# Chunk loop of a hybrid SSD and DeltaNet block: state-space output computed by channels, corners only in the last substitution steps, decay rows requested from ScalarE

## The chip, the cores and the metric

One core of a Trainium2 chip runs the whole kernel. The metric is the device time in microseconds; for the kernel before it is the median of three runs. A profile of one execution goes with it.

## The reference

One layer (`DEPTH` = 1) on 1024 tokens of 1024 channels, all in float32. Only the part around the change is kept here.

```python
def ssd_chunked(xh, dt, a, bm, cm):                      # 16 heads of 64, 2 groups, state 128
    a_cum = jnp.cumsum(a_dt, axis=-1)
    lmat = jnp.exp(jnp.where(causal, a_cum[..., :, None] - a_cum[..., None, :], -jnp.inf))
    scores = jnp.einsum('bclgn,bcsgn->bcgls', cc, bc)
    y_diag = jnp.einsum('bcgrls,bcsgrp->bclgrp', scores[:, :, :, None] * lmat, xc)
    ...                                                  # states carried from chunk to chunk
    y_off = jnp.einsum('bclgn,bcgrpn,bcgrl->bclgrp', cc, prev, jnp.exp(a_cum))
    return (y_diag + y_off).reshape(bsz, s, h, pd)

# mamba2_branch: y = (y + d_skip * xh) * silu(z), then an RMS norm per group
# gated_delta_chunked, 8 heads of 128:
    sol = lax.linalg.triangular_solve(t_mat, rhs, left_side=True, lower=True, unit_diagonal=True)
    v_new = u_c - w_c @ state
    o = qd_c @ state + qk_c @ v_new
    state = state * last_c + kd_c.T @ v_new

# around it: proj = h @ w_in; two branch projections merged by sigmoid gates; w_out; a gated
# conv-MLP with D_FF = 4096; a gated per-layer input embedding; RMS norms between them
```

The kernel uses chunks of 128 tokens in place of 64; the recurrences give the same result.

## The kernel before

The program is written by hand for five engines, each with its own instruction stream; semaphores tie them together. `wait_ge` puts a wait in front of the next instruction of an engine. There is no scheduler: the order of the work is the order of the code. The helper `after(eng, s, count)` (L861) waits for a count of a semaphore that earlier stages have used already.

The large products (`w_in`, the branches, the MLP) are done as three fp32r products of a high and a low part, each 128x512; they fill most of the time. TensorE has such products through the chunk loop too: `gemm(steps)` (L1054) puts in steps of six of them, from the projection for the merge gates, between the small products of a chunk. A chunk has 12 steps in chunks 0 to 3 and 8 in chunks 4 to 7.

The chunk loop handles 8 chunks of 128 tokens (`NCH`). For a chunk `c`:

- SyncE (`sp_mixer`) requests all inputs: `gt` (gates), `qk`, `xbc` (x, B and C by channels), `bv`, `dec`, `kdec`, `mq`, `zt` (silu of z), and for the chunk after next `nt` and `dd`. `dec` is a broadcast: 16 rows of 128 cumulated decays are read for each of the 128 partitions (L921), 1 MB in pieces of 512 B.
- GpSimd (`pool_mixer`) subtracts the own token's sum from `dec` and masks it (`decays`, L988), scales x (`decayed_x`), decays the states, puts the skip term into `yssm` (`skip_x`), and splits weights.
- ScalarE (`act_mixer`) takes the exponential of `dec`, copies PSUM results (`rhs`, `rinv`, `bs`), squares, and has the Ln/Exp pairs for the norms. `mg_evict` takes a finished gate tile out of PSUM.
- VectorE (`dve_mixer`) multiplies `dec` with the scores (L1320), forms `rhs`, sums outputs and states, and multiplies by the norm factors (L1378 for the DeltaNet heads, L1384 for the state-space channels).
- TensorE (`pe_mixer`) does products of 8 or 16 heads at a time through the PSUM banks `PA`, `PB`, `PC` (two each).

The triangular solve is an inverse by blocks of 32. The inverses of the diagonal blocks come from an earlier stage (`dd`). In the loop, `invert_r` forms one factor `rinv`, and `invert_h` / `invert_x` apply it three times, each time 8 products of 128x128 on TensorE and two additions on VectorE (L1313), so that the blocks further from the diagonal fill in one step at a time.

The state-space output of a chunk is formed by tokens: `off_done` marks C times the state (L1121), which VectorE scales by the exponential of the sum (L1346) into `ysum`; `diag` (L1097) multiplies the masked scores of 8 heads with x, with two neighbouring heads' channels as the moving operand, half of which is thrown away by `add_diag` (L1322). It runs twice, since 8 heads fill the two banks. TensorE then transposes `ysum` (L1151) to channels, and VectorE adds it to `yssm` (L1369) and multiplies by `zt` (L1372).

The numbers of instructions that the text uses are those of the lines below.

## Time and profile before

| | |
|---|---|
| runs | 2536.34, 2541.39, 2546.09 us; median 2541.39 |
| span of the profiled execution | 2534.6 us |
| time of the profiled execution beyond its span | the profile gives none |
| busy: TensorE, VectorE, ScalarE, GpSimd | 96%, 61%, 32%, 50% |
| chunk loop with its start (740 to 1130 us) | 390 us of the span |

The span is the time from the first to the last instruction of one profiled execution; it is 6.8 us below the median of the runs. "Busy" adds up the time in which an engine works on something. A line such as `[0.64 <-DVE rhs L1337]` in the timeline says that the engine sat idle for 0.64 us before the instruction and that line 1337 on VectorE released it. Stretches are given in microseconds from the start of the span.

### The profile page before, as it was taken

The numbers are of one execution on the slowest core, as the hardware profiler recorded it, in microseconds if no ns is written. First come the engines' busy times: TensorE is split into PE (matmuls) and PEld (weight loads), VectorE is DVE, ScalarE is ACT, GpSimd is POOL, SyncE is SP. The second block draws the span as 40 slices with busy tenths as digits, with TensorE's granted clock in tenths as the row PEclk, the third lists the DMA queues.
The fourth block names the chain that finished last, engine by engine and source line by source line (L and its number), as shares of the span: only waits on it lengthen the run. The fifth ranks groups of instructions, "written<-read, shape, count | busy, mean of one in ns | idle before, by whom it ended". The sixth has DMA issues, their size and how long they took to land. (4 is left out here: it accounts for less than half of the span.)

```text
span 2534.6 us, 29658 instructions
## 1 busy us (share of the span) xinstructions
PE 2436.9 (96%) x11540; PEld 2011.4 (79%) x11540; DVE 1538.6 (61%) x1411; ACT 822.5 (32%) x965; POOL 1266.1 (50%) x687
## 2 busy tenths in 40 slices
PE   7999999899999999989999899999999999999998
PEld 6888887677778888878878678888888878888776
DVE  4977997325766567653244897677677652323575
ACT  5234443445412232331013543333333321000332
POOL 2337887544445455443353266556556543333563
PEclk9999999999999999999999999999999999999999
DMA  6222334698676667745232222222222243122332
GB/s 230 92 84 92 108 120 135 216 267 283 202 209 168 187 173 215 178 141 174 100 133 83 100 83 75 74 98 75 74 97 76 100 174 116 50 83 84 131 101 108
DMA packets 293607, 335.34 MB, mean 132 GB/s; under 512 B 44461, under 2 KB 249594, under 8 KB 289402
## 3 DMA queue, kind: packets, MB, share of 16 engines
q1 hardware_dynamic: 260650, 271.42, 34.4%
q10 hardware_dynamic: 32848, 62.40, 6.7%
q8 instruction: 76, 1.25, 0.2%
q14 instruction: 33, 0.27, 0.0%
HBM read 230.50 MB, written 103.28 MB: 132 GB/s over the span
## 5 line engine op out<-in xcount | busy, mean ns | idle before, releaser
L498 PE MATMUL ps<-act_hi,w_hi 128*128 128x512 f32 x1328 | 532.4, 401 | 13.3 <-ACT ring_b L1212 4.8
L483 POOL TENSOR_SCALAR w_hi<-w_raw 128x1024 fp32r<-128x1024 f32 x123 | 145.0, 1179 | 764.0 <-issue 688.4
L502 PE MATMUL ps<-act_hi,w_lo 128*128 128x512 f32 x1328 | 518.4, 390 | 0.0
L501 PE MATMUL ps<-act_lo,w_hi 128*128 128x512 f32 x1328 | 517.9, 390 | 0.0
L485 POOL TENSOR_TENSOR w_lo<-w_raw,w_hi 128x1024 fp32r<-128x1024 f32 x123 | 328.6, 2672 | 10.3
L498 PEld LDWEIGHTS ps<-act_hi,w_hi 128*128 128x128 f32 x1328 | 250.0, 188 | 71.6 <-issue 8.1
L502 PEld LDWEIGHTS ps<-act_hi,w_lo 128*128 128x128 f32 x1328 | 249.8, 188 | 53.1
L501 PEld LDWEIGHTS ps<-act_lo,w_hi 128*128 128x128 f32 x1328 | 250.1, 188 | 52.3 <-issue 3.3
L2036 POOL TENSOR_TENSOR w_lo<-sm,w_hi 128x512 fp32r<-128x512 f32 x120 | 209.1, 1743 | 113.9 <-ACT w_hi L2390 113.9
L2036 POOL TENSOR_TENSOR w_lo<-w_raw,w_hi 128x512 fp32r<-128x512 f32 x90 | 139.3, 1549 | 151.8 <-ACT w_hi L2390 151.8
L2152 PE MATMUL ps<-t,w_hi 128*128 128x512 f32 x480 | 186.9, 389 | 0.2 <-POOL w_lo L2036 0.2
L2153 PE MATMUL ps<-t,w_hi 128*128 128x512 f32 x480 | 186.8, 389 | 0.0
L2154 PE MATMUL ps<-t,w_lo 128*128 128x512 f32 x480 | 186.7, 389 | 0.0
L2152 PE MATMUL ps<-act_hi,w_hi 128*128 128x512 f32 x360 | 140.3, 390 | 3.2 <-DVE ring L2716 2.7
L2153 PE MATMUL ps<-act_lo,w_hi 128*128 128x512 f32 x360 | 140.1, 389 | 0.0
L2154 PE MATMUL ps<-act_hi,w_lo 128*128 128x512 f32 x360 | 140.1, 389 | 0.0
L2799 DVE TENSOR_TENSOR tile<-ps,tile 128x1024 f32<-128x1024 f32 x24 | 29.4, 1224 | 160.8 <-PE ps L502 133.8
L2390 ACT ACTIVATE w_hi<-sm 128x512 fp32r<-128x512 f32 x120 | 75.3, 630 | 133.0 <-PE ps L2154 133.0
L2464 ACT ACTIVATE act_hi<-f_raw 128x1024 fp32r<-128x1024 f32 x32 | 31.2, 1047 | 254.7 <-DMA f_raw<-f_cm 254.7
L579 POOL TENSOR_TENSOR w_lo<-csm,w_hi 128x512 fp32r<-128x512 f32 x48 | 93.3, 1953 | 34.6 <-ACT w_hi L648 34.5
L2152 PEld LDWEIGHTS ps<-t,w_hi 128*128 128x128 f32 x480 | 90.1, 188 | 19.3 <-POOL w_lo L2036 0.6
L2153 PEld LDWEIGHTS ps<-t,w_hi 128*128 128x128 f32 x480 | 90.1, 188 | 18.7
(393 smaller groups left out, 5130.9 us busy)
## 6 DMA issues: line engine op xcount, KB each, us to landing
w_raw<-in_w_in_dram SPq DMA_DIRECT2D x34, 1024.0 KB, 6.0
spill<-ring_a ACTq DMA_DIRECT2D x36, 512.0 KB, 2.6
w_raw<-in_w_ffn_down_dram SPq DMA_DIRECT2D x18, 1024.0 KB, 5.0
w_raw<-in_w_ffn_up_dram SPq DMA_DIRECT2D x16, 1024.0 KB, 5.2
w_raw<-in_w_ffn_gate_dram SPq DMA_DIRECT2D x16, 1024.0 KB, 5.2
f_cm<-ring SPq DMA_DIRECT2D x32, 512.0 KB, 2.6
spill<-ring_b ACTq DMA_DIRECT2D x31, 512.0 KB, 6.9
qkv_a<-spill SPq DMA_DIRECT2D x7, 1536.0 KB, 8.4
```

Source lines behind the costliest of these rows:

```text
L483: nc.gpsimd.tensor_scalar(hi, raw, 1.0, 0.0, ALU.mult, ALU.add).then_inc(split_done, 1)
L485: nc.gpsimd.tensor_tensor(lo, raw, hi.bitcast(f32), ALU.subtract).then_inc(split_done, 1)
L498: first = nc.tensor.matmul(o, wh, mov[0][:, k, c], start=(k == 0), stop=False)
L501: nc.tensor.matmul(o, wh, mov[1][:, k, c], start=False, stop=False)
L502: last = nc.tensor.matmul(o, wl, mov[0][:, k, c], start=False, stop=(k == KD - 1))
L579: nc.gpsimd.tensor_tensor(c_slot(w_lo, j), c_product_in(p, i), c_slot(w_hi, j).bitcast(f32), ALU.subtract).then_inc(c_low[0], 1)
L2036: nc.gpsimd.tensor_tensor(product_slot(w_lo, j), product_in(q, i), product_slot(w_hi, j).bitcast(f32), ALU.subtract).then_inc(w_low[0], 1)
L2152: nc.tensor.matmul(dst, wh[:, k, :], mh[:, k, :], start=(k == 0), stop=False)
L2153: nc.tensor.matmul(dst, wh[:, k, :], ml[:, k, :], start=False, stop=False)
L2154: last = nc.tensor.matmul(dst, wl[:, k, :], mh[:, k, :], start=False, stop=(k == 3))
L2390: a(product_slot(w_hi, j), product_in(q, i), ACT.Copy).then_inc(w_high[0], 1)
L2464: a(hi[:, k, :], raw[:, k, :], ACT.Copy).then_inc(f_hi_done, 1)
```

## The change

Four edits, all in the chunk loop or for it:

1. The state-space output is formed by channels. C times the state (now `s_ssm` of two heads as the stationary operand) gives channels by tokens, in 8 products. `diag` has the x of one head (64 channels) as the stationary operand and the masked scores as the moving one, even heads to PSUM partitions 0 to 63, odd heads to 64 to 127. All 16 heads fit into the two banks at once, so `diag` runs once, and the eight transposes of `ysum` go. VectorE multiplies by the exponential of the sums with channels on partitions, which needs these rows broadcast: a second scratch tensor `exp_rows` is written once before the loop, and SyncE loads it into `zt` ahead of each chunk's output (two transfers); `zt` is loaded a second time in the chunk, with z, once the product has been formed.
2. The second and third substitution step compute only the corner of the matrix that still changes, 64x64 and 32x32 per head, and VectorE copies the corner instead of adding the whole.
3. `dec` for the next chunk is requested by ScalarE, after the second `rhs` copy, once `diag` is done.
4. The semaphore counts follow (`x_step` 4 instead of 6 a chunk, `diag_done` 1 instead of 2, `y_sum` 2 instead of 3).

```diff
+    CORNER = {1: (slice(0, 64), 64), 2: (slice(0, 32), 32)}
+
+    def load_dec(eng, c):
+
+        after(eng, diag_done, c)
+        eng.dma_start(dec[:, :, :], cum_rows[ROW_DT:ROW_DT + SSM_HEADS, tokens(c)].unsqueeze(0).broadcast_to([P, SSM_HEADS, P])
+                      ).then_inc(in_dec, 16)
...
+        def load_e(c):
+            after(sp, y_mid, c * 2)
+            for i in range(2):
+                rows = exp_rows[ROW_DT + i:ROW_DT + SSM_HEADS:2, tokens(c)]
+                sp.dma_start(zt[64 * i:64 * i + 64, :, :], rows.unsqueeze(0).broadcast_to([64, KD, P])).then_inc(in_e, 16)
 
         def load_z(c):
-            after(sp, y_mid, c * 2)
+            after(sp, y_sum, c * 2 + 1)
             sp.dma_start(zt[:, :, :], spill_c[:, J_Z:J_Z + Z_T, tokens(c)]).then_inc(in_z, 16)
...
                 load_qk(c + 1)
                 load_xbc(c + 1)
                 load_bv(c + 1)
+            load_z(c)
             if c in blocks_at:
                 block_load(blocks_at[c])
             if c < NCH - 1:
-                load_dec(c + 1)
                 load_kd(c + 1)
                 load_mq(c + 1)
-                load_z(c + 1)
+                load_e(c + 1)
...
+            after(pe, x_step, c * 4 + nth + 1)
+            rows, n = CORNER[nth]
+            for h in range(GDN_HEADS):
+                last = t.matmul(bank(PB + nth - 1)[rows, h * n:(h + 1) * n], rinv[:, h, rows], xinv[:, h, P - n:P], start=True, stop=True)
+            last.then_inc(h_done, 1)
...
-        def diag(c, g):
-            for i in range(HPG):
-                h = g * HPG + i
-                last = t.matmul(bank(PB, 2)[:, i * P:(i + 1) * P], dec[:, h, :],
-                                xc[:, h - h % 2:h - h % 2 + 2, :].rearrange("p h d -> p (h d)"), start=True, stop=True)
+        def diag(c):
+            for h in range(SSM_HEADS):
+                d = slice(SSM_HEAD_DIM * (h % 2), SSM_HEAD_DIM * (h % 2) + SSM_HEAD_DIM)
+                last = t.matmul(bank(PB, 2)[d, h // 2 * P:(h // 2 + 1) * P], xc[:, h, :], dec[:, h, :], start=True, stop=True)
             last.then_inc(diag_done, 1)
...
-            after(pe, o_sum, c * 2 + 2)
-            for k in range(KD):
-                last = t.transpose(bank(PA, 2)[:, k * P:(k + 1) * P], ysum[:, k * P:(k + 1) * P], ident[:, :])
-            last.then_inc(yt_done, 1)
...
+            if more:
+                load_dec(act, c + 1)
             after(act, o_sum, c * 2 + 2)
...
+            if nth:
+                rows, n = CORNER[nth]
+                after(dve, h_done, c * 4 + nth + 2)
+                after(dve, x_step, c * 4 + nth + 1)
+                v.tensor_copy(xinv[rows, :, P - n:P], bank(PB + nth - 1)[rows, 0:GDN_HEADS * n].rearrange("p (h t) -> p h t", t=n)
+                              ).then_inc(x_step, 1)
+                return
...
-            v.tensor_tensor(hd(ysum[:, :]), hd(bank(PC, 2)), wide(head_cols(c, EXP_D, SSM_HEADS), SSM_HEAD_DIM),
-                            ALU.mult).then_inc(y_sum, 1)
-            after(dve, y_sum, c * 3 + 1)
-            add_diag(c, 0)
-            add_diag(c, 1)
+            after(dve, in_e, c * 32 + 32)
+            after(dve, y_mid, c * 2)
+            v.tensor_tensor(hd(ysum[:, :], KD), hd(bank(PC, 2), KD), zt[:, :, :], ALU.mult).then_inc(y_sum, 1)
+            after(dve, diag_done, c + 1)
+            after(dve, y_sum, c * 2 + 1)
+            v.tensor_tensor(ysum[:, :], bank(PB, 2), ysum[:, :], ALU.add).then_inc(y_sum, 1)
...
+            a(hrow[:, 0, :], hrow[:, 1, :], ACT.Exp).then_inc(tm_act, 1)
+            act.wait_ge(tm_act, 5)
+            act.dma_start(exp_rows, hrow[:, 0, :]).then_inc(cum_kept, 16)
```

How the streams stand. On TensorE, in a chunk of the second half of the loop, from the products with `rhs` (L1068, the new values) over `diag` (L1100) to the state update; before:

```order
L1068 MATMUL ps<-rhs,xinv 128x128 x8
L1100 MATMUL ps<-xc,dec 128x128 x8
L498 MATMUL ps<-act_hi,w_hi 128x512
L501 MATMUL ps<-act_lo,w_hi 128x512
L502 MATMUL ps<-act_hi,w_lo 128x512
L498 MATMUL ps<-act_hi,w_hi 128x512
L501 MATMUL ps<-act_lo,w_hi 128x512
L502 MATMUL ps<-act_hi,w_lo 128x512
L1100 MATMUL ps<-xc,dec 128x128 x8
L1068 MATMUL ps<-rhs,kdec 128x128 x8
```

and in the changed kernel, where `diag` is L1115 and the helper for products by head L1078:

```order
L1078 MATMUL ps<-rhs,xinv 128x128 x8
L1115 MATMUL ps<-dec,xc 64x128 x16
L499 MATMUL ps<-act_hi,w_hi 128x512
L502 MATMUL ps<-act_lo,w_hi 128x512
L503 MATMUL ps<-act_hi,w_lo 128x512
L499 MATMUL ps<-act_hi,w_hi 128x512
L502 MATMUL ps<-act_lo,w_hi 128x512
L503 MATMUL ps<-act_hi,w_lo 128x512
L1078 MATMUL ps<-rhs,kdec 128x128 x8
```

The sixteen products stand together, with 64 stationary columns each; the step of large products follows them. Further on in the same chunk, from the sum of squares (L1166) over the second and third substitution step to the transposes of the DeltaNet output (L1176); before:

```order
L1166 MATMUL ps<-sqs,ones 128x128 x8
L1068 MATMUL ps<-xinv,rinv 128x128 x8
L498 MATMUL ps<-act_hi,w_hi 128x512
L501 MATMUL ps<-act_lo,w_hi 128x512
L502 MATMUL ps<-act_hi,w_lo 128x512
L498 MATMUL ps<-act_hi,w_hi 128x512
L501 MATMUL ps<-act_lo,w_hi 128x512
L502 MATMUL ps<-act_hi,w_lo 128x512
L1068 MATMUL ps<-xinv,rinv 128x128 x8
L1176 MATMUL ps<-ident,qs 128x128 x8
```

and in the changed kernel (L1096 is the corner product, L1176 the sum of squares, L1186 the transposes):

```order
L1176 MATMUL ps<-sqs,ones 128x128 x8
L1096 MATMUL ps<-xinv,rinv 64x64 x8
L499 MATMUL ps<-act_hi,w_hi 128x512
L502 MATMUL ps<-act_lo,w_hi 128x512
L503 MATMUL ps<-act_hi,w_lo 128x512
L499 MATMUL ps<-act_hi,w_hi 128x512
L502 MATMUL ps<-act_lo,w_hi 128x512
L503 MATMUL ps<-act_hi,w_lo 128x512
L1096 MATMUL ps<-xinv,rinv 32x32 x8
L1186 MATMUL ps<-ident,qs 128x128 x8
```

The order is the same, the two steps are smaller. On SyncE, the requests of one chunk with no weight block among them, before:

```order
L931 DMA gt<-spill 128x8x128
L899 DMA qk<-gdn_in 128x2048
L909 DMA xbc<-spill 128x12x128
L903 DMA bv<-gdn_in 128x1024
L921 DMA dec<-cum_rows 128x16x128
L913 DMA kdec<-gdn_in 128x1024
L917 DMA mq<-gdn_in 128x1024
L926 DMA zt<-spill 128x8x128
```

and in the changed kernel, where `dec` stands in ScalarE's stream between the `rhs` copies and the square of `qs`:

```order
L941 DMA gt<-spill 128x8x128
L908 DMA qk<-gdn_in 128x2048
L918 DMA xbc<-spill 128x12x128
L912 DMA bv<-gdn_in 128x1024
L936 DMA zt<-spill 128x8x128
L922 DMA kdec<-gdn_in 128x1024
L926 DMA mq<-gdn_in 128x1024
L932 DMA zt<-exp_rows 64x8x128 x2
```

z now follows `bv`, in the chunk that uses it, and the broadcast of the exponentials stands last.

## Rows read from the trace of the kernel before

**Rows 1.** The page, busy time, share of the span and instructions.

```profile
PE 2436.9 (96%) x11540; PEld 2011.4 (79%) x11540; DVE 1538.6 (61%) x1411; ACT 822.5 (32%) x965; POOL 1266.1 (50%) x687
```

**Rows 2.** Windows: length, busy time by engine, granted clock, DMA share, GB/s.

```profile
700.00:767.00 67.00, 61.29 (x301) 51.68 (x299) 44.95 (x72) 10.27 (x10) 26.24 (x14) 0.97 0.63 183
767.00:1094.00 327.00, 313.50 (x2121) 275.43 (x2120) 217.37 (x212) 97.85 (x118) 177.25 (x72) 1.00 0.68 185
1094.00:1130.00 36.00, 29.32 (x154) 24.23 (x154) 12.50 (x13) 8.28 (x10) 5.97 (x4) 0.91 0.33 109
```

**Rows 3.** Waits of PE, 740 to 1130 us: total, times, longest.

```profile
PE ps L1176 <- DVE qs L1378: 6.2, 5, 2.2
PE ps L498 <- ACT ring_b L1212: 4.8, 4, 2.5
PE ps L1068 <- DVE rhs L1337: 4.4, 6, 1.1
```

**Rows 4.** Timeline of PE in chunk 2: start, length, engine, line, what.

```profile
869.68 1.95 PE L1100 MATMUL ps<-xc,dec 128*128 128x128 f32 x16
871.39 0.48 PE L498 MATMUL ps<-act_hi,w_hi 128*128 128x512 f32 x1
...
885.84 1.04 PE L1151 MATMUL ps<-ident,ysum 128*128 128x128 f32 x8
886.63 0.47 PE L498 MATMUL ps<-act_hi,w_hi 128*128 128x512 f32 x1
...
897.32 1.95 PE L1068 MATMUL ps<-xinv,rinv 128*128 128x128 f32 x16
899.02 0.47 PE L498 MATMUL ps<-act_hi,w_hi 128*128 128x512 f32 x1
```

**Rows 5.** Timeline of chunk 5, from one set of new values to the next.

```profile
1006.15 1.16 PE L1068 MATMUL ps<-rhs,xinv 128*128 128x128 f32 x8 [0.64 <-DVE rhs L1337]
...
1023.27 1.23 DVE L1372 TENSOR_TENSOR yssm<-yssm,zt 128x1024 f32<-128x1024 f32 x1
1024.53 1.06 ACT L1247 ACTIVATE sqs<-yssm 128x1024 f32<-128x1024 f32 x1 [2.79 <-DVE yssm L1372]
...
1027.91 1.95 PE L1166 MATMUL ps<-sqs,ones 128*128 128x128 f32 x16
1029.70 1.95 PE L1068 MATMUL ps<-xinv,rinv 128*128 128x128 f32 x16
...
1032.39 1.88 DVE L1378 TENSOR_TENSOR qs<-qs,orst 128x1024 f32<-128x1024 f32 x1
...
1034.65 1.04 PE L1176 MATMUL ps<-ident,qs 128*128 128x128 f32 x8
...
1048.41 1.16 PE L1068 MATMUL ps<-rhs,xinv 128*128 128x128 f32 x8 [0.67 <-DVE rhs L1337]
```

**Rows 6.** DMA issues: count, KB each, us to landing; loop, then windows 831:832, 1000:1002.

```profile
dec<-cum_rows SPq DMA_DIRECT2D x7, 1024.0 KB, 17.5
...
spill<-ring_b ACTq DMA_DIRECT2D x1, 512.0 KB, 14.9
...
spill<-ring_b ACTq DMA_DIRECT2D x1, 512.0 KB, 2.8
```

**Rows 7.** Window in which dec's broadcast alone is under way, chunk 5.

```profile
1015.00:1027.00 12.00, 12.00 (x84) 10.39 (x84) 8.69 (x10) 3.59 (x5) 0.00 (x0) 1.00 0.58 77
```

**Rows 8.** Timeline of SyncE's queue in chunk 5.

```profile
1008.64 0.74 SPq L903 DMA_DIRECT2D bv<-gdn_in  x1
1012.66 0.36 SPq L921 DMA_DIRECT2D dec<-cum_rows  x1
```

**Rows 9.** Lines L1378 and L1313 on DVE: ns min/median/max.

```profile
L1378 DVE TENSOR_TENSOR qs<-qs,orst x8: 1224/2469/4527, 807.9 to 1116.1; 128x1024 f32<-128x1024 f32 x8
...
L1313 DVE TENSOR_TENSOR xinv<-ps,dd x48: 673/690/694, 753.7 to 1077.8; 128x512 f32<-128x512 f32 x48
```

**Rows 10.** Timeline of DVE where the decay sums are written out, before the loop.

```profile
157.55 2.29 DVE L3270 TENSOR_TENSOR ct_raw<-ct_raw,act_hi 128x2048 f32<-128x2048 f32 x1
```

73 lines of the change are left out of this document (32 added, 41 removed).

## The prediction

> **What bounds the kernel now.** I read the busy line of the page first: TensorE works for 96% of the span, no other engine more than 61% [rows 1]. Then the windows by stage: in the chunk loop (767 to 1094 us) TensorE is busy for 313.5 of 327 us, at a granted clock of 1.00, which is the level of 2.4 GHz; in the last chunk's tail 29.3 of 36 us [rows 2]. So a microsecond taken from TensorE inside the loop is a microsecond of the whole, unless a wait takes its place. Third, TensorE's waits in the loop. The largest three are small in sum, 6.2, 4.8 and 4.4 us, but all three lie in one chain of a chunk: the transposes of the DeltaNet output wait for VectorE's L1378, the gate tile waits for ScalarE to empty it, the new values wait for `rhs` [rows 3]. In the second half of the loop, where a chunk has only 8 steps of large products, this chain is as long as TensorE's work. One chunk there takes 1048.41 - 1006.15 = 42.3 us [rows 5]. Fourth, the transfers, because the change touches their order: the DMA share is 0.68 in the loop [rows 2], and the broadcast of `dec` needs 17.5 us to land [rows 6]. While it is alone it moves only 77 GB/s [rows 7], against 185 on average [rows 2]; this transfer is slow by itself.
>
> **The change part by part.**
>
> *Transposes of ysum.* Eight of them hold TensorE for 886.63 - 885.84 = 0.79 us [rows 4]; in 8 chunks 6.3 us. They have no wait in front, so all of it counts.
>
> *C times the state.* Two products of 512 columns become eight of 128: the same number of columns moved. I count 0. VectorE's sum over PSUM has the same number of elements as before.
>
> *diag.* Eight products take 871.39 - 869.68 = 1.71 us [rows 4], sixteen 3.42. The changed kernel has sixteen as well, with 128 moving columns each, but each takes only half of the array's columns. No row of this kernel shows such a pair. Lower bound of the gain: nothing overlaps, and the array has to run empty where its shape changes, twice a chunk. The group of eight lasts 1.95 us while the next starts after 1.71 [rows 4], so a tail of 0.24 us is hidden today and would be exposed: a loss of 0.5 us a chunk. Upper bound: the pairs overlap fully, 1.71 us a chunk. I take overlap with both tails, 1.71 - 0.5 = 1.2 us, in 8 chunks 9.7 us: the two heads share no operand and no output, so nothing in the program orders them.
> The Trainium skill (TensorEngine Tiling (Array Packing), sections Overview and Key Properties) says that tiles of 64 columns give up to 2x and can load weights and multiply in parallel, and that a change of the tiling mode drains the engine. By the first, the sum is as above. By the second alone, with no overlap, this term is -4 us instead of +9.7. No row before the change tells which.
>
> *Corners.* A full step takes 899.02 - 897.32 = 1.70 us [rows 4]. With 64 and 32 of 128 columns, the two are 0.85 and 0.43 us if the time follows the columns: 2.1 us saved, less four exposed tails of 0.24, 1.2 us a chunk. But what is late next stands right behind them. In chunk 5 the sum of squares ends at 1029.70; VectorE starts L1378 2.7 us later, when ScalarE has its factors, and the transposes follow at 1034.65, 4.95 us after [rows 5]. TensorE's work in between (two steps and a step of large products) fills this today, just; shortened to some 3.2 us, it waits for L1378 instead. The wait of [rows 3] grows by what the corners save. What can make it shorter is L1378 itself: 1.22 us at its fastest, 2.47 at the median [rows 9], slow while GpSimd works on `dec` at the same time. I count 0.4 us a chunk for 7 chunks, 2.8 us (bounds 0 and 1.2 us a chunk), and 1 us before chunk 0, where no such wait follows. VectorE loses four additions of 0.69 us [rows 9] and gets two copies of some 0.7 and 0.4 us, by their elements: 1.7 us off VectorE, of which about 1 us lies in the chain behind L1378 (the third step). In chunks 4 to 6, where the gate tile and `rhs` are waited for, I count this 1 us; in chunks 0 to 3 TensorE has work there.
>
> *The request of dec, and z.* `dec` was requested at 1012.66 [rows 8], when the second `diag` was done. Now it can go about 3 us earlier, and it no longer stands behind `xbc` and `bv` in SyncE's queue. But those, and z, are then under way at the same time. How a broadcast on one queue treats the other is in the trace: a store of 512 KB that ScalarE issued at about the time of a `dec` broadcast needed 14.9 us, the same store with no broadcast 2.8 us [rows 6]. z is now requested after `bv`, at about 1009.5, and was requested a chunk ahead before. VectorE wants it at 1023.27 [rows 5], some 2 us earlier after the savings. At full speed it is there by 1016; starved, it lands when the broadcast ends: 1 MB at 77 GB/s is 13.6 us [rows 7], from about 1011, plus what is left, 1027.5. I take 1026. From z to the sum of squares there are 2.5 us (1023.27 to the end of the square at 1025.6, and a hand-over) [rows 5], so TensorE gets it at 1028.5, against 1027.91 - 0.79 - 1.2 = 1025.9 without the delay: 2.6 us lost in each of chunks 4 to 6. In chunks 0 to 3 the step is covered by more large products, in chunk 7 there is no `dec`; 0 there.
> The Trainium skill (DMA: Bandwidth & Descriptors, section Issuing engines are not separate DMA queues) says that transfers from ScalarE and SyncE run on the same 16 engines and that a second issuer saves only the issue time. By it `dec` lands no earlier than before; the slowed store agrees that the two share something.
>
> *The broadcast of the exponentials.* 0.5 MB at 77 GB/s is 6.8 us of the same slow kind, requested after VectorE is done with z (about 1024.5), wanted near 1049. It is covered by 18 us; if it were not, VectorE's L1360 and the state update behind it would wait.
>
> *Before the loop.* One exponential more on ScalarE and a second store, for which VectorE waits before L3270 at 157.55 [rows 10]: up to 3 us late. TensorE has no wait in that stage and tiles in reserve. I count 0, bound 3.
>
> **The sum.** Chunks 0 to 3: 0.8 + 1.2 + 0.4 = 2.4, times 4 = 9.6. Chunks 4 to 6: 2.4 + 1.0 - 2.6 = 0.8, times 3 = 2.4. Chunk 7: 0.8 + 1.2 = 2.0. Before chunk 0: 1. Together 15.0 us. Against the profiled execution this is a span of 2534.6 - 15.0 = 2519.6. The profiled span stood 6.8 us below the median of the runs, so the time is 2541.4 - 15.0 = 2526 us.
>
> **The rivals.**
>
> 1. *No overlap in diag.* The halves of the array take turns. The term goes from +1.2 to -0.5 a chunk, 13.7 us; in chunks 4 to 6, where z is late, 5.1 of these are hidden. Gain 15.0 - 13.7 + 5.1 = 6.4, 2535 us. For it: no row shows an overlap. Against it: nothing in the program's waits.
> 2. *z in time, and L1378 free of GpSimd.* If the queues share fairly, z lands by 1023.5 and the 2.6 us are not lost: 7.8 us. If `dec` then lands 3 us earlier, L1378 may run at 1.22 us, 1.2 us less than its median, in 7 chunks up to 8: gain 28 to 30, 2512 us. Against it: the slowed store.
> 3. *The transfers become the bound, slower than before.* The loop's DMA share is 0.68 [rows 2], the second broadcast adds 6.8 us of slow traffic a chunk. If it does not fit between the others, chunks 4 to 6 each grow by it and chunks 0 to 3 by half of it: 20.4 + 13.6 - 15.0 = +19, 2560 us. It decides once the loads of a chunk of 42 us together need longer than the chunk; today some 13 us are free of them (0.32 of 42).
> 4. *dec lands no earlier.* By the skill's rule above, taken as a mechanism of this kernel: `dec` arrives as before, L1378 stays slowed, and the 2.8 us go: 2529 us.
>
> **How the numbers follow.** Forecast 0.45 (its own range 2519 to 2533), rival 1 0.25, rival 2 0.13, rival 3 0.10, rival 4 0.07. A change of under 0.5%, 12.7 us, is about what a measurement of this kernel cannot tell from none: it needs a time below 2528.7 or above 2554.1. Below lie 0.7 of the forecast, all of rival 2 and a little of 1 and 4: 0.50. Above lies most of rival 3: 0.08. Range: 2510 (rival 2) to 2545 (rival 1 with 3 us before the loop and the scatter of the runs).
>
> **What would show it.** In the changed profile sixteen `diag` products should take about 2 us instead of 3.4 (3.4 or more is rival 1). The wait of the transposes for L1378 should grow to 1 to 2 us a chunk. VectorE should wait for z in chunks 4 to 6 and not in 0 to 2; no such wait is rival 2. `dec` should land 2 to 5 us earlier in its chunk; if not, rival 4. A wait for the exponentials, or a DMA share above 0.9 in the loop, is rival 3. The prediction is wrong at its root if the chunks of the first half do not get shorter by about 2 us each.

## The result and the profile after

The changed kernel took 2548.4 us (median of 20 runs; 20 runs of the kernel before on the same chip: 2538.8). The ratio is 1.0036, 95% interval 1.0026 to 1.0046: 9 us slower, where 15 us faster were forecast. The profiled execution lasted 2548.7 us with a span of 2547.0. One profile of each kernel is compared in what follows; the runs of the changed kernel lie between 2540.3 and 2554.8 us.

The windows of the trace after, in the columns of [rows 2] for TensorE alone (busy, granted clock, DMA share, GB/s), answer to those rows:

```profile
700.00:767.00 67.00, 58.53 (x276) 0.95 0.68 208
767.00:1094.00 327.00, 292.83 (x2174) 0.97 0.72 190
1094.00:1130.00 36.00, 26.52 (x156) 0.91 0.36 112
```

In the window of the loop TensorE is busy for 292.8 us where it was 313.5 (over the whole span 2416.2 against 2436.9); the work is gone as promised. By form (busy us, mean ns), after:

```profile
L1115 PE MATMUL ps<-dec,xc 128*64 128x128 f32 x256 | 15.7, 275 | 0.8
...
L1096 PE MATMUL ps<-xinv,rinv 128*64 128x64 f32 x128 | 9.2, 225 | 0.0
L1096 PE MATMUL ps<-xinv,rinv 128*32 128x32 f32 x128 | 5.5, 197 | 0.0
```

Before, these were 31.5 us for `diag` and 31.2 for the two later steps of `invert_h`, and 8.3 for the transposes of `ysum`. But idle time has come in its place. TensorE's waits from 740 to 1145 us, against [rows 3]:

```profile
PE ps L499 <- ACT ring_b L1222: 28.4, 5, 7.6
PE ps L499 <- POOL w_lo L486: 7.1, 1, 7.1
PE ps L1186 <- DVE qs L1391: 6.1, 3, 2.5
PE ps L1078 <- DVE rhs L1350: 5.0, 6, 1.6
```

The wait for the gate tile (`mg_evict`, L1222) has grown from 4.8 us to 28.4, and the wait for L1391, which I had expected to grow, has not. Behind the gate tile stands `dec`. The waits of GpSimd, ScalarE and VectorE for it in the loop:

```profile
POOL dec L1002 <- DMA dec<-cum_rows: 134.8, 7, 21.7
```
```profile
ACT dec L1240 <- POOL dec L1004: 57.4, 6, 12.1
```
```profile
DVE dec L1339 <- ACT dec L1240: 34.1, 4, 10.3
```

Before, the first two were 117.3 and 30.0 us and the third did not exist: in the kernel before, VectorE never waits for `dec`. The issues with KB each and median us to landing, against 17.5 for `dec` in [rows 6]:

```profile
dec<-cum_rows ACTq DMA_DIRECT2D x7, 1024.0 KB, 21.5
w_raw<-in_w_in_dram SPq DMA_DIRECT2D x5, 1024.0 KB, 17.3
...
zt<-spill SPq DMA_DIRECT2D x8, 512.0 KB, 8.1
```

One slow passage, from chunk 1 to chunk 2. First the requests, on SyncE and then ScalarE (the products of `diag` end at 830.9):

```profile
832.23 0.37 SPq L918 DMA_DIRECT2D xbc<-spill  x1
832.65 0.73 SPq L912 DMA_DIRECT2D bv<-gdn_in  x1
833.43 0.42 SPq L936 DMA_DIRECT2D zt<-spill  x1
833.90 1.64 SPq L456 DMA_DIRECT2D w_raw<-in_w_in_dram  x1
835.66 3.35 SPq L922 DMA_DIRECT2D kdec<-gdn_in  x1
```
```profile
835.21 1.02 ACT L1222 ACTIVATE ring_b<-ps 128x1024 f32<-128x1024 f32 x1
836.27 0.34 ACTq L1224 DMA_DIRECT2D spill<-ring_b  x1
836.65 0.54 ACTq L889 DMA_DIRECT2D dec<-cum_rows  x1
```

`dec` is requested 5.8 us behind the last product that reads it, since ScalarE evicts a gate tile first, and `bv`, z, the weight block and `kdec`, 2.5 MB, have been asked for just ahead of it. In the kernel before, SyncE did this in the same place:

```profile
824.36 0.36 SPq L909 DMA_DIRECT2D xbc<-spill  x1
824.78 0.97 SPq L903 DMA_DIRECT2D bv<-gdn_in  x1
825.80 0.42 SPq L455 DMA_DIRECT2D w_raw<-in_w_in_dram  x1
830.49 0.36 SPq L921 DMA_DIRECT2D dec<-cum_rows  x1
```

There `dec` went out with the last product, z was not asked for until 13 us later, and the block had 4.7 of the 8.3 us that it took behind it. Then what follows in the kernel after: GpSimd, ScalarE, VectorE, TensorE.

```profile
860.54 3.61 POOL L1002 TENSOR_TENSOR dec<-dec,tmc 128x2048 f32<-128x2048 f32 x1 [19.20 <-DMA dec<-cum_rows]
864.23 4.50 POOL L1004 TENSOR_TENSOR dec<-dec,m_incl 128x2048 f32<-128x2048 f32 x1
```
```profile
868.76 1.91 ACT L1240 ACTIVATE dec<-dec 128x2048 f32<-128x2048 f32 x1 [12.11 <-POOL dec L1004]
...
870.68 1.28 ACT L1222 ACT_TABLE_LOAD   x1
871.98 1.02 ACT L1222 ACTIVATE ring_b<-ps 128x1024 f32<-128x1024 f32 x1
```
```profile
870.70 3.94 DVE L1339 TENSOR_TENSOR dec<-dec,bs 128x1024 f32<-128x1024 f32 x2 [10.32 <-ACT dec L1240]
874.56 0.68 DVE L1347 TENSOR_TENSOR rhs<-ps,tmc 128x512 f32<-128x512 f32 x1
875.27 1.68 DVE L1350 TENSOR_TENSOR rhs<-bv,rhs 128x512 f32<-128x512 f32 x1
```
```profile
873.06 0.79 PE L499 MATMUL ps<-act_hi,w_hi 128*128 128x512 f32 x1 [7.55 <-ACT ring_b L1222]
...
877.49 1.05 PE L1078 MATMUL ps<-rhs,xinv 128*128 128x128 f32 x8
879.31 1.16 PE L1078 MATMUL ps<-rhs,xinv 128*128 128x128 f32 x8 [0.77 <-DVE rhs L1350]
880.60 1.97 PE L1115 MATMUL ps<-dec,xc 128*64 128x128 f32 x32
```

This is a closed ring through the one buffer `dec`: the diagonal products end, `dec` is requested, lands, GpSimd passes over it twice, ScalarE takes the exponential, VectorE masks it and then forms `rhs`, TensorE makes the new values and the next diagonal products. A second leg runs beside it: exponential, gate tile, large products. Besides, the granted clock is lower behind the wait of 7.55 us, 0.61 on average from 873.0 to 877.5: the first of the large products there follow each other at 0.43 us (the level of 1.2 GHz), the last at 0.23 (2.4 GHz), and the twelve take 4.4 us (873.06 to 877.49) instead of 2.7.

Means over the seven passages between chunks, worked out from the timelines of one execution each (us; "land" is from the request to GpSimd's start; "exp to mask" holds the exponential, 1.9, and what VectorE still does first; "mask to diag" runs to the first diagonal product):

| kernel | request late | land | GpSimd to exp | exp to mask | mask to diag | diag | ring |
|---|---|---|---|---|---|---|---|
| before | 0.0 | 17.5 | 8.7 | 3.8 | 9.1 | 6.0 | 45.0 |
| after | 1.7 | 21.0 | 9.0 | 2.5 | 9.6 | 2.0 | 45.7 |

In the kernel before only 3.8 - 1.9 = 1.9 us of the ring is slack on average: 3.1 us in the first four passages, 0.25 in the last three. VectorE goes straight from its other work to the masking there, so the ring is close to binding and does not bind. The change takes 4.0 us out of it at `diag` and puts 5.1 in at the request and the landing. In the changed kernel VectorE waits for `dec` in four of the seven passages, 34.1 us together; in these the ring does bind.

VectorE and GpSimd meet in a second way, which the ring does not show. In the kernel before, between chunks 5 and 6, a VectorE pass of 128x1024 takes 4.2 us and ends one microsecond behind GpSimd's pass over `dec`:

```profile
1035.56 4.21 DVE L1384 TENSOR_TENSOR yssm<-yssm,sqs 128x1024 f32<-128x1024 f32 x1
```
```profile
1033.27 5.42 POOL L994 TENSOR_TENSOR dec<-dec,m_incl 128x2048 f32<-128x2048 f32 x1
```

The same pass took 1.72 us at 903.43, beside shorter passes of GpSimd, and in the changed kernel (L1397) 1.20 at 857.98, with none beside it. So when GpSimd works on `dec` also decides how long VectorE's passes take, whether or not anybody waits for `dec`.

Ahead of the loop the first diagonal product of chunk 0 has slipped from 777.5 to 784.3 us. Two places make this. At 160.74 us VectorE has waited 2.4 us where it did not wait before [rows 10]; the profile names no releaser, and the wait that the code has there is the one for the store of the exponentials. Its second pass takes 4.37 us where it took 3.02, beside GpSimd's weight splits in both kernels, and further on TensorE waits for such a split, which it did not before:

```profile
160.74 2.86 DVE L3286 TENSOR_TENSOR ct_raw<-ct_raw,act_hi 128x2048 f32<-128x2048 f32 x1 [2.43 <-issue]
163.63 4.37 DVE L3286 TENSOR_TENSOR ct_raw<-ct_raw,act_lo 128x2048 f32<-128x2048 f32 x1
```
```profile
PE ps L612 <- POOL w_lo L580: 2.9, 1, 2.9
```

At the large products that follow the sums of `hrow` (L1438, was L1425) TensorE is 5.1 us late (679.4 against 674.3). And the two broadcasts of the exponentials stand ahead of chunk 0's weight block on SyncE: GpSimd waits 14.0 us for the block, was 8.4, and TensorE then 7.1 for GpSimd, was 1.6. This last wait is 5.1 to 11.0 us in the traces of all variants of the changed kernel below, and 1.5 to 2.8 in those of the kernel before. The first diagonal product comes at 779.0 to 793.2 us in the former and at 770.3 to 777.5 in the latter, so the late start is not chance. From the first to the last diagonal product the loop takes 319.9 us, was 315.2; the last group itself is 3.2 us shorter. Of the 4.1 us behind the loop, 2.4 arise at 1320 us. Both kernels have two short waits there (1.8 and 1.0 us before, 1.8 and 0.6 here), and the granted clock from 1320 to 1330 us is 0.68 here and 1.00 before. In the experiments below the stretch from 1300 to 1360 us has a clock between 0.94 and 1.00 in variants of either kernel (0.94 in the kernel before with the short ring, 1.00 with the corners), so I put that down to chance and not to the change; no run shows what decides it.

### The profile page after: what moved, and what is told of

Its sections match the earlier page's. It is cut to its first block and busy times, and to the rows that moved or that the text cites. A ratio compares the mean times of both kernels' runs of the same rounds, so it can differ in the third digit from the quotient of the medians.

```text
span 2547.0 us, 29691 instructions
## 1 busy us (share of the span) xinstructions
PE 2416.2 (95%) x11572; PEld 1988.0 (78%) x11572; DVE 1527.2 (60%) x1387; ACT 822.7 (32%) x966; POOL 1261.7 (50%) x687
## 5 line engine op out<-in xcount | busy, mean ns | idle before, releaser
L499 PE MATMUL ps<-act_hi,w_hi 128*128 128x512 f32 x1328 | 535.6, 403 | 43.3 <-ACT ring_b L1222 28.4
L486 POOL TENSOR_TENSOR w_lo<-w_raw,w_hi 128x1024 fp32r<-128x1024 f32 x123 | 334.0, 2716 | 10.3
L2477 ACT ACTIVATE act_hi<-f_raw 128x1024 fp32r<-128x1024 f32 x32 | 31.2, 1048 | 254.6 <-DMA f_raw<-f_cm 254.6
```

The lines of the kernel that those rows point to most:

```text
L486: nc.gpsimd.tensor_tensor(lo, raw, hi.bitcast(f32), ALU.subtract).then_inc(split_done, 1)
L499: first = nc.tensor.matmul(o, wh, mov[0][:, k, c], start=(k == 0), stop=False)
L2477: a(hi[:, k, :], raw[:, k, :], ACT.Copy).then_inc(f_hi_done, 1)
```

## The experiments

Ratios are to the kernel before, run on the same chip as the variant; the changed kernel is at 1.0036. Differences between variants are taken from the ratios, since not all ran on the same chip.

**What delays dec.** First, `dec` on SyncE at its old place, all else changed.

```diff
-            if more:                      # act_mixer
-                load_dec(act, c + 1)
+                load_dec(sp, c + 1)       # sp_mixer, behind block_load
```

> The changed kernel with one part undone: dec's broadcast is requested by SyncE behind the weight block again, before kdec. Theory A (dec's broadcast, requested from ScalarE, shares the DMA engines with the weight block, lands 4 us later, GpSimd and then ScalarE's exponential are late, and the gate tile's eviction behind that exponential keeps TensorE from bank 0): dec's median landing goes back to 17 to 18 us, the exponential's wait for GpSimd from 57 us to about 30, the four waits of L499 for the gate tile of 5.4 to 7.6 us go to under 3 us each, the clock in 767:1094 is 0.99 or 1.00, and the time is 15 to 25 us below the changed kernel's 2548. Theory B (the exponentials' broadcast and z's new place load the DMA engines so that dec is late from whichever queue it comes): dec still lands at 20 us or more, the waits stay, and the time is within 5 us of the changed kernel.

Ratio 1.0009 [0.9998, 1.0019], 2542.0 us: 7 us better, but by neither theory. Landings stayed at 20 us on average and requests 1.8 us late, since z, which waits for VectorE, now stands ahead of block and `dec`. So the queue alone is not the point; the runs below vary what goes out beside `dec` and ahead of it.

Second, the request from ScalarE ahead of its eviction.

```diff
-            if c in (1, 3):
-                mg_evict({1: 3, 3: 6}[c])
             if more:
                 load_dec(act, c + 1)
+            if c in (1, 3):
+                mg_evict({1: 3, 3: 6}[c])
```

> The changed kernel with ScalarE's request of dec put ahead of the gate tile's eviction in chunks 1 and 3. The runs so far make the ring of dec the bound of the loop: diagonal products end, dec is requested, lands (17 to 24 us), GpSimd 8 us, exponential 2, VectorE's masking 5, diagonal products again. Theory A (the ring): in chunks 1 and 3 the request goes out 0.1 us behind the last diagonal product instead of 5.7 us behind it; the rings 1 to 2 and 3 to 4 shorten by 4 to 6 us each, and the time is 8 to 12 us below the changed kernel's (ratio to before about 0.999 to 1.001). Theory B (the DMA engines' load sets when dec lands): dec asked for earlier lands no earlier, because weight block, z and kdec move the same bytes in that stretch; the rings shorten by less than 2 us and the time by less than 4.

1.0019 [1.0006, 1.0033]. The request is on time (0.04 us), the landing 0.7 us longer (21.7), the ring 45.4. The gain of 4 us lies within the overlap of the intervals. By the time B is nearer, by the rings that it named A is: from chunk 1 to 2 and from 3 to 4 they shortened by 3.7 and 4.6 us (51.7 to 48.0, 49.5 to 44.9), but others grew, the first from 44.6 to 46.8, as `dec` landed later there.

Third, on top of it, the weight block behind everything else.

```diff
-            if c in blocks_at:
-                block_load(blocks_at[c])
             if c < NCH - 1:
                 load_kd(c + 1)
                 load_mq(c + 1)
                 load_e(c + 1)
+            if c in blocks_at:
+                block_load(blocks_at[c])
```

> As the kernel with dec's request ahead of the eviction on ScalarE, and the weight block of each chunk requested last, behind the exponentials' broadcast, so that it no longer shares the DMA engines with dec. Theory A (the block costs dec 3 to 5 us in the chunks that have one: 21.8, 23.9, 19.9, 21.7, 23.6 us against 17.1 and 19.0): all landings are 17 to 19 us, the rings of those chunks shorten by 3 to 4 us more, and the time is 2518 to 2530, below both kernels. Theory B (z, 512 KB right behind the diagonal products, is what dec shares with): landings of 20 us or more remain and the time is within 3 us of the same kernel with the block at its place; or the block is now late for GpSimd's splits, which would show as GpSimd waits for w_raw of 3 us or more.

0.9994 [0.9978, 1.001], 2536.2 us: the loss is gone, the hoped-for gain isn't there, and neither theory's numbers came (landings are 20.2 on average, ring 44.1, 6 us better than without the move). VectorE's wait for `dec` is 8.8 us, was 34.1. In this execution the loop takes 309.0 us from the first to the last diagonal product, 6.2 less than in the kernel before, and the late start (783.0) takes 5.5 of them back.

Fourth, z cut to an eighth (the rest left out).

```diff
-            sp.dma_start(zt[:, :, :], spill_c[:, J_Z:J_Z + Z_T, tokens(c)])
+            sp.dma_start(zt[:, 0:1, :], spill_c[:, J_Z:J_Z + 1, tokens(c)])
```

> The changed kernel with z's load cut to one of its eight rows of tiles (64 KB instead of 512 KB; the other seven are left out, so the gated output is not the reference's). It tells apart what makes dec's landing late. Theory A (z, requested 5 us behind the diagonal products where before it came at the end of the chunk's loads, moves 512 KB in dec's window): median landing falls from 21.5 us to 18 to 19.5, exponential's wait for GpSimd falls below 45 us, time 6 to 12 us below the changed kernel's. Theory B (the weight block and kdec, which SyncE no longer holds back behind dec, are what dec shares with): landings stay at 20.5 to 22 us and the time is within 4 us.

1.0004 [0.9991, 1.0017]: 8 us less, as theory A has it. The issue rows give

```profile
dec<-cum_rows ACTq DMA_DIRECT2D x7, 1024.0 KB, 17.9
```

VectorE's wait for `dec` falls from 34.1 to 14.0 us. So z's 512 KB in dec's window cost, and its removal gives back most of the loss. The weight block's part is less sure: put last together with the earlier request it gave back 11 us, but the step from the one to the other (1.0019 to 0.9994) lies within overlapping intervals. The broadcast of the exponentials and `kdec` also go out beside `dec`; no run took them away.

Fifth, `dec` on SyncE behind the block, and z behind `dec`.

```diff
                 load_dec(sp, c + 1)
+            load_z(c)
+            if c < NCH - 1:
                 load_kd(c + 1)
```

> The changed kernel with dec requested by SyncE at its old place behind the weight block, and z, which waits for VectorE's last addition to the state-space output, behind dec instead of ahead of it. The first run with dec on SyncE took 2542 us with requests 4.7 us behind the diagonal products in chunk 1 (z's wait is ahead of it in SyncE's stream) and landings of 20 to 23 us, against 16 to 18 in the kernel before. Theory A (z, ahead of dec in the queue, costs the ring both its wait and its 512 KB): landings go back to 16 to 18 us, requests to 0.1 us, each ring shortens by 3 to 6 us until TensorE bounds the chunk at 41 to 43 us, and the time is 2520 to 2532, below both kernels. Theory B (the landing is slow for the exponentials' broadcast): landings stay at 20 us or more and the time is within 4 us of 2542.

1.0083 [1.006, 1.0107]: both theories fell. Now z is late, and TensorE waits on the chain behind it:

```profile
PE ps L1178 <- DVE xc L1316: 46.5, 7, 10.5
```
```profile
DVE yssm L1385 <- DMA zt<-spill: 60.3, 7, 10.5
```

The z term of the forecast exists, then, where z has to follow `dec` in the queue. With `dec` on ScalarE it shows too, smaller: VectorE waits for z 13.5 us in the second run above and 10.1 in the third, and not in the changed kernel.

**Who waits for dec.** The exponential behind the output stores and the gate tile:

```diff
-            if more:
-                exp_dec(c + 1)
             after(act, y_out, c + 1)
             ...
             if c in (1, 3, 4, 5, 6):
                 mg_evict({1: 4, 3: 7, 4: 8, 5: 9, 6: 10}[c])
+            if more:
+                exp_dec(c + 1)
```

> The changed kernel with ScalarE's exponential of dec moved behind the two output stores and the gate tile's eviction of its chunk; dec's request stays on ScalarE. Theory A (the eviction stands behind a late exponential): the four waits of L499 of 5.4 to 7.6 us go to under 2.5 us each though dec lands as late as before the move, about 18 us of idle and some 5 us of slower clock go, the time is 10 to 20 us below the changed kernel's; one table load more per chunk costs ScalarE 1.3 us, and the masked scores start 1 to 3 us later. Theory B (the wait is only passed on: masked scores late, the C times state group and the diagonal products wait for them instead): L1115 waits 2 to 5 us for VectorE in those chunks and the time is within 5 us of the changed kernel.

1.0135 [1.0118, 1.0152], 2574 us. The waits for the gate tile went (2.2 us in all), and more of another kind came:

```profile
PE ps L1078 <- DVE rhs L1350: 41.0, 9, 7.2
```

GpSimd to exponential rose by 6.2 us a passage and the ring by 3.7, to 49.4; seven times 3.7 are the 26 us that the time grew by. Neither theory had this time. In the changed kernel, what is put into the ring comes out as time, and the gate tile is not the cause but a second leg.

Masking behind `rhs` on VectorE, in the changed kernel, with all mended places, and in the kernel before with the corners:

```diff
                 v.tensor_tensor(rhs[:, h, :], bv[:, h, :], rhs[:, h, :], ALU.subtract).then_inc(r_step, 1)
+            mix_scores(c)
...
-            if more:
-                mix_scores(c + 1)
```

> The changed kernel with VectorE's masking of dec moved behind the four operations that make the right-hand side (rhs), so that the DeltaNet products which stand ahead of the diagonal ones on TensorE no longer wait for dec. Theory A (the ring of dec bounds the chunk: last diagonal product, dec's request, landing of 17 to 24 us, GpSimd 8.2, exponential 1.9, masking 3.9, rhs 3.8 to 4.7, DeltaNet products and diagonal products 4): rhs's 4 us leave the ring, the waits of L1078 for rhs go to under 1 us in all, but the wait for the gate tile's eviction behind the exponential stays; chunks shorten by 1 to 3 us and the time is 6 to 16 us below the changed kernel's. Theory B (the gate tile's eviction alone sets the end in the slow chunks and TensorE in the others): the diagonal products begin no earlier and the time is within 4 us of the changed kernel's.

> The changed kernel with four edits together: dec's request ahead of the eviction on ScalarE, the weight block last, the exponential of the running sums early before the pair stage, masking behind rhs. Theory A (each takes its own part out of the ring or of the way to it): 2515 to 2528, ratio 0.991 to 0.996, the chunk's period 41 to 42.5 us on average against 44.1 with the first two alone, so that TensorE's shorter work at last shows in the time. Theory B (the gate tile's eviction or z's late landing is the next bound at about 44 us a chunk): 2532 to 2538.

> The kernel before with the corner substitution and with masking behind rhs; nothing else of the change. The corners alone took 9 us out of TensorE's busy time and gave 2 us. Theory A (the ring of dec, 41 to 45 us in the kernel before too, is what kept the rest): with rhs out of the ring the chunk's period falls from 45 to 43 or less, and the time is 8 to 16 us below the kernel before (0.994 to 0.997). Theory B (the corners' gain is lost to the chain on VectorE, L1392 into the transposes, 12.4 us of waits in that run): within 4 us of the corners alone, 2536.

1.0065 [1.0048, 1.0083], 1.0029 [1.0017, 1.0041] and 1.0032 [1.0021, 1.0044]: slower than the same kernels without the edit in the first and third (1.0036 and 0.9992) and outside both theories in all three, so I had the order wrong. Where `dec` is in time, the masking filled VectorE's time before the first products of the chunk were there; behind them, the diagonal products wait for it (L1107 waits 14.9 us in the third, none before).

TensorE's large products behind the diagonal ones, with three of the mended places, against these three alone:

```diff
             last.then_inc(off_done, 1)
-            gemm(steps[0])
...
             diag(c)
-            gemm(steps[1])
+            gemm(steps[0] + steps[1])
```

> The changed kernel with three edits: dec's request ahead of the eviction on ScalarE, the weight block last, the exponential of the running sums early. Theory A (the head's 2.5 to 5 us and the loop's 12 us are separate): 2531 to 2535, ratio 0.997 to 0.999. Theory B (the head's gain doesn't add to the loop's): 2535 to 2538, ratio 0.999 to 1.000.

> The same three edits, and on TensorE the gate gemm steps between the C times state group and the DeltaNet products moved behind the diagonal products. Theory A (where dec is late, the ring runs over the gate tile's eviction: exponential, table load, eviction, gemm 2.7 to 4 us, DeltaNet products, diagonal products): the waits of L499 for the eviction go, diagonal products follow masking and rhs directly, 1 to 3 us off the ring per chunk, and the time is 3 to 10 us below the three edits alone. Theory B (those gemm steps cover TensorE's wait for rhs): L1078 now waits 2 to 4 us for VectorE's rhs in each chunk, at a lower clock behind it, and the time is 5 to 20 us above.

The three: 1.001 [0.9996, 1.0024], above both theories, though B lies within the interval; the early exponential added nothing to the two edits before it (0.9994). With the edit: 1.0064 [1.0046, 1.0082], 14 us more, as theory B has it but not for its reason. The wait for `rhs` did not come (0.3 us), and `dec` landed in 18.6; but what needs the earlier transfers now came sooner than they did:

```profile
PE ps L1102 <- DMA xbc<-spill: 40.2, 6, 10.6
```
```profile
DVE yssm L1384 <- DMA zt<-spill: 66.7, 7, 13.3
```

**What TensorE's work is worth.** Even heads first, then the odd ones:

```diff
-            for h in range(SSM_HEADS):
+            for h in [*range(0, SSM_HEADS, 2), *range(1, SSM_HEADS, 2)]:
```

> The changed kernel with the diagonal products in another order: the eight even heads (columns 0 to 63 of the array) first, then the eight odd heads, so that no two neighbours can run side by side. Theory A (neighbours on the two halves of the array overlap fully): the 16 products of a chunk take 3.9 us instead of 2.0, TensorE's busy time rises by 13 to 16 us, and the time is 8 to 16 us above the changed kernel's. Theory B (the products got shorter for another reason, or the stage waits for VectorE anyway): busy time rises by less than 5 us or the time by less than 3.

The products take 3.3 us a chunk in place of 2.0, so neighbours on the two halves overlap:

```profile
L1115 PE MATMUL ps<-dec,xc 128*64 128x128 f32 x256 | 26.4, 275 | 0.9
```

TensorE's busy time rose by 9.5 us, less than theory A's 13 to 16, and the ratio is 1.0048 [1.0029, 1.0066]: 3 us, not told from none, as B has it.

The kernel before with the corners alone (`invert_h` and `invert_x` of the change):

> The kernel before with only the corner substitution of the change (products of 64 and 32 columns and two copies instead of four batches of whole products with two additions of 128 by 1024 each). It takes about 16 us of TensorE's work out of the loop and nothing else. Theory A (dec's ring has 3 to 5 us of slack in each chunk of the kernel before, beside TensorE): the chunks shorten by 1 to 3 us each until the ring bounds them, and the time is 8 to 16 us below the kernel before (ratio 0.994 to 0.997). Theory B (the ring bounds the kernel before already): within 4 us of it.

0.9992 [0.9978, 1.0006], 2536.3 us. TensorE works 9.0 us less, the ring stays at 45.0 and the time moves 2 us, not told from none. This is B's number, and it refutes the forecast's assumption. It does not show B's reason: VectorE waits for `dec` as little as before. What grew is TensorE's wait for VectorE's norm, by 6.2 us from the 6.2 of [rows 3]:

```profile
PE ps L1183 <- DVE qs L1392: 12.4, 7, 2.9
```

And the norm's next pass (L1398, was L1384), which lies beside GpSimd's passes over `dec`, takes 27.1 us in all, was 20.7.

**The ring made shorter** (GpSimd's subtraction for one head of 16):

```diff
-            g.tensor_tensor(dec[:, :, :], dec[:, :, :], wide(head_cols(c, CUM_D, SSM_HEADS), P), ALU.subtract)
+            g.tensor_tensor(dec[:, 0:1, :], dec[:, 0:1, :], wide(head_cols(c, CUM_D, 1), P), ALU.subtract)
```

> The kernel before with GpSimd's first pass over dec done for one head of 16 (15 left out). Theory A (ring and TensorE are about equally long in the kernel before): TensorE's busy share in the loop is 0.96 already, so the time falls by only 2 to 8 us, and the changed kernel with the same pass shortened is 5 to 12 us below this one: there the change is worth what its shorter TensorE work promised. Theory B (the change costs time for another reason than the ring, such as the load on the DMA engines alone): the changed kernel stays above this one by 5 us or more.

> The changed kernel with GpSimd's first pass over dec (subtraction of the running sums, 3.6 us) done for one head of 16; the other 15 are left out, so the decays are not the reference's. It takes 3.4 us out of the ring of dec in each chunk and touches nothing else, except that VectorE has GpSimd beside it for less long. Theory A (the ring bounds the changed kernel): the chunk's period falls from 45.7 to 42 to 43 on average and the time is 15 to 25 us below the changed kernel's. Theory B (TensorE's own order, evictions and transfers bound it): within 5 us.

The kernel before: 0.9948 [0.9934, 0.9962]; the changed one: 0.997 [0.9957, 0.9983]. So 3 us less of GpSimd's work a passage gives 13 us in the one and 17 in the other, where 9 us less of TensorE's work gave 2. In the first, TensorE then does bound the loop:

```profile
767.00:1094.00 327.00, 321.37 (x2197) 1.00 0.68 187
```

For this one theory A named 2 to 8 us. The edit does two things at once, though: it shortens the ring, and it takes GpSimd away from beside VectorE. In the kernel before no wait for `dec` on VectorE was there to be saved. VectorE's own passes got shorter, and the slack of the ring grew, from 1.9 to 3.3 us. Two of the passes in the kernel before, and then with GpSimd's short one:

```profile
L1320 DVE TENSOR_TENSOR dec<-dec,bs 128x1024 f32<-128x1024 f32 x16 | 28.7, 1833 | 0.0
L1384 DVE TENSOR_TENSOR yssm<-yssm,sqs 128x1024 f32<-128x1024 f32 x8 | 20.7, 2591 | 0.0
```
```profile
L1320 DVE TENSOR_TENSOR dec<-dec,bs 128x1024 f32<-128x1024 f32 x16 | 21.0, 1348 | 0.0
L1384 DVE TENSOR_TENSOR yssm<-yssm,sqs 128x1024 f32<-128x1024 f32 x8 | 14.9, 1865 | 0.0
```

These 13.5 us are as many as the kernel gained, so the run does not show that the ring bound the kernel before; it shows that GpSimd's pass cost time, through the ring or through VectorE. For the changed one A holds, and there the ring is seen: the masking stays as it was (28.8 and 28.9 us), and VectorE's wait for `dec` falls from 34.1 to 22.1. But the changed kernel stays 5.6 us above the kernel before with the same short pass (the intervals just overlap), where theory A of that run had it 5 to 12 below; that is its theory B. Both loops then take 304 us from the first to the last diagonal product, with 43.4 us a passage: what `diag` saves (3.9) is again spent on the request and the landing (1.7 and 2.6).

> The kernel before with the corner substitution, and GpSimd's first pass over dec done for one head of 16 (15 left out). The corners took 9 us out of TensorE's work and gave 2 us with the whole ring. Theory A: with the short ring they give 5 to 9 us: 0.991 to 0.993 of the kernel before, against 0.9948 without the corners. Theory B (VectorE's chain, whose wait at L1183 was 12 us with the corners, takes it): 0.994 to 0.996.

> The changed kernel with dec's request ahead of the eviction, the weight block last and the early exponential, and GpSimd's first pass over dec done for one head of 16 (15 left out). Theory A (TensorE's saved work counts once dec's ring is out of the way): 0.987 to 0.992 of the kernel before, 8 to 20 us below the kernel before with the same pass shortened, periods of 39 to 42 us. Theory B (the next bound, VectorE's chain to L1186 or the eviction, is as long as the old one): 0.994 to 0.996, no better than the kernel before with the short pass.

Corners under the short ring: 0.9939 [0.9925, 0.9954]; its medians, 2519.2 against 2538.0, would say 0.9926. Against 0.9948 without the corners the intervals overlap, so whether the corners pay there is not settled. The changed kernel with three places mended: 0.9993 [0.9974, 1.0013], single runs from 2520 to 2546. It is no better than the kernel before with the short pass, as theory B says, but above its 0.994 to 0.996 and not with the bound it named: the loads are next. TensorE waits for `xbc` (9.3 us, 2 times), VectorE for z (22.7 us, 5 times), and one passage took 50 us.

**The head.** The exponential of the sums and its store ahead of the other four:

```diff
             act.dma_start(cum_rows, hrow[:, 1, :]).then_inc(cum_kept, 16)
+            a(hrow[:, 0, :], hrow[:, 1, :], ACT.Exp).then_inc(tm_act, 1)
+            act.wait_ge(tm_act, 1)
+            act.dma_start(exp_rows, hrow[:, 0, :]).then_inc(cum_kept, 16)
             a(tmh[:, :, TM_BETA, :], lb, ACT.Exp).then_inc(tm_act, 1)
```

> The changed kernel with the exponential of the running sums and its store ahead of the four other exponentials before the pair stage, so that VectorE's wait for the store (2.4 us at 158 us) is covered. Theory A (4 to 5 of the 12 us that the profiled execution is longer come from this wait, which shifts VectorE's 2048-element passes under GpSimd's weight splits): the wait at 158 us goes to under 0.5 us, the first pair product starts at 198 us instead of 201.1, and the time is 3 to 5 us below the changed kernel's. Theory B (the shift at 200 us is absorbed or comes from noise between executions): the first pair product is early but the time is within 1.5 us of the changed kernel's.

1.0026 [1.0017, 1.0036]: 2.5 us by the ratios, within their overlap and between the theories. VectorE's wait fell to 0.84 us but its long passes and the 2.9 us wait of L612 stayed. In this execution the loop starts at 779.0 us, with the three edits together at 784.1. No run put the broadcasts behind chunk 0's weight block, so what that wait costs (6.1 us here) was not tested.

## Why the prediction was wrong

1. *"A microsecond taken from TensorE inside the loop is a microsecond of the whole, unless a wait takes its place."* This is the step that failed: waits did take the place, and the sum had next to nothing for them. TensorE's work in the loop fell by 20.7 us, and in its place came a wait of 28.4 us for the gate tile (was 4.8) at a lower clock, behind a `dec` for which VectorE now waits 34.1 us (was none). TensorE's 96% [rows 1] hid a ring across five engines and a transfer that was 1.9 us from binding on average. The rows for it stood there ([rows 6] with 17.5 us, one buffer); I looked at each wait by itself and never added the ring up. By its own test the forecast is wrong at the root: the four passages of the first half took 46.4, 45.8, 47.0 and 45.9 us and take 44.6, 51.7, 42.7 and 49.5. For the changed kernel this is shown: taking z away gave 8 us back, the request and the block moved 11, and 3.7 us a passage put in cost 26. In the kernel before TensorE's time was not free for the taking either (the corners alone gave 2 us of 9), but there no engine but GpSimd and ScalarE waited for `dec`; how much of that is VectorE's chain and how much GpSimd's passes beside it stays open.
2. *The removed work.* Right. Transposes 6.3 us forecast, 8.3 busy; `diag` forecast 1.2 us a chunk: the next product starts 1.90 us behind the first of sixteen (880.60 to 882.50) against 3.42, so 1.5, near the upper bound. The Trainium skill's "up to 2x" (TensorEngine Tiling (Array Packing), Overview) is fully reached: 31.5 to 15.7 us busy. Corners 1.2 us a chunk forecast of TensorE's time, 2.1 before tails: 31.2 - 14.7 = 16.5 us busy over eight chunks, and by the starts (948.61 to 949.68, 951.27 to 952.02) 1.8 us in place of 3.4, so 1.6 a chunk. C times the state 15.3 to 15.7: right.
3. *The wait for L1378 takes the corners' gain.* In the changed kernel it did not grow (6.2 to 6.1). But the mechanism was right: where `dec` is not so late, the wait is there, 12.4 us with the corners alone, 11.3 with an eighth of z, 14.2 with the block last.
4. *dec 3 us earlier, z 2.6 us late.* Both the other way round: `dec` needs 3.5 us longer to land and is asked for up to 5.8 us late, z is in time. I had reckoned what `dec` does to z and not what z, block and `kdec` do to `dec`. The Trainium skill says that both issuers use the same 16 engines (DMA: Bandwidth & Descriptors, Issuing engines are not separate DMA queues). This case agrees as far as it goes: `dec` took 21.0 us from ScalarE's queue and 20.1 from SyncE's. My rival 4 took from it "lands as before", too mild. Rival 3 had the sign and the loads, but the DMA share is 0.72, not 0.9: here a transfer in a ring cost time with the engines a good quarter idle.
5. *The broadcast of the exponentials, 0.* In the loop nobody waits for it, but it is under way while `dec` lands, and what that costs was not tested. Wrong for chunk 0, where it stands ahead of a weight block that is waited for.
6. *Before the loop, 0, bound 3.* The second term that was mis-sized: the loop starts 6.8 us late in the profiled execution, 5.1 of them before 680 us. The first part differs from execution to execution; the wait behind chunk 0's weight block is in all traces of the changed kernel.

The forecast of 2526 us missed by 22, and of the rivals only the third, at 0.10, had the sign. Together, in the profiled span: 6.8 us of late start, 4.7 between the first and the last diagonal product, 3.2 less for the shorter last group, and 4.1 behind the loop make the 12.4 us.

No version that computes everything beats the kernel before by more than the measurement can tell; the block last (0.9994) and the corners alone (0.9992) equal it.

## What to carry to other kernels

Before costing a microsecond of the busiest engine, follow each single-buffered tile once round, from its last reader through request, landing and every engine to that reader again, and compare the sum with the loop's period. If it is within a few per cent, work taken off the busiest engine elsewhere may be worth little, and the bytes that go out beside the tile's load can cost time. Then see which engine really waits for the tile: in the kernel before none on TensorE's path did, and in the changed one VectorE did. When a request is moved, list what leaves within its landing time, not only what queues with it.

## What the runs showed of the hardware

- Two 64-column products on the halves of the array run side by side: sixteen take 2.0 us in turn and 3.3 with even heads first; sixteen of 128 columns took 3.4.
- A 1 MB broadcast to 128 partitions with 2.5 MB of other loads asked for just ahead took 23.9 us to GpSimd's start. In the two passages of the changed kernel without a weight block it took 17.1 and 19.0. The weight block that was asked for 4.7 us ahead of the broadcast took 8.3 us (kernel before); asked for beside it, 17.3 at the median of five.
- VectorE's passes take longer beside GpSimd's: L1384 4.21 us when 3.1 of them lay beside GpSimd's L994, and 1.20 (L1397 of the changed kernel) with no GpSimd pass; the first masking pass (L1320) 3.30 at 906.27, all of it beside GpSimd, and 1.21 at 861.44 with no GpSimd pass.
